# Even-layer forget sums: one scan over 512 tokens for all heads, one product per head over 128 rows

## What is computed

```
logf = log_sigmoid(f_logit + b_f)                  # (token, head)
c    = cumsum(logf, over tokens)
s    = q k^T / 8 + c[query] - c[key]               # causal
y    = softmax(s) v
```

## Time and profile before

| what | value |
|---|---|
| median of 3 runs | 2528.32 us (2528.26 to 2529.1) |
| the profiled execution: its own time | 2530.0 us |
| its span in the trace | 2528.2 us |
| PE busy | 2433.6 us, 96% |
| DVE busy | 1658.5 us, 66% |
| ACT busy | 1168.0 us, 46% |
| mean granted clock of PE | 0.989 |

### The profile page before, as it was taken

One profiled execution on the slowest core, in us unless ns is written; L12 is line 12 of the kernel. 1 busy time (PEld: TensorE's weight loads), 2 busy tenths in 40 slices (PEclk: granted clock), 3 DMA queues, 4 the chain that ended last, 5 costly groups with the idle time before them and its releaser, 6 DMA issues.

```text
span 2528.2 us, 37287 instructions
## 1 busy us (share of the span) xinstructions
PE 2433.6 (96%) x13811; PEld 2151.9 (85%) x13811; DVE 1658.5 (66%) x2733; ACT 1168.0 (46%) x2111; POOL 146.7 (6%) x217
## 2 busy tenths in 40 slices
PE   7999999999999999999999999999988899999998
PEld 5999987886777899987789998777777677999887
DVE  6777647666666877745687774563235868777545
ACT  4455435344445555534545553452223655555444
POOL 1000001100002000001000000100001420000000
PEclk9999999999999999999999999999997999999999
DMA  4333334421304233334423323443244042333345
GB/s 132 98 84 84 109 124 164 117 73 52 111 19 126 74 89 92 89 124 132 159 70 91 92 85 125 133 146 125 79 125 117 9 142 72 93 87 84 108 133 175
DMA packets 259138, 261.87 MB, mean 104 GB/s; under 512 B 25568, under 2 KB 214000, under 8 KB 258977
## 3 DMA queue, kind: packets, MB, share of 16 engines
q1 hardware_dynamic: 254224, 243.83, 31.9%
q0 software_dynamic: 4464, 14.80, 1.7%
q10 hardware_dynamic: 288, 1.10, 0.1%
HBM read 249.11 MB, written 10.58 MB: 103 GB/s over the span
## 4 chain that ended last, share of the span: by engine, by line
PE 83%; DVE 9%; ACT 3%; issue 2%; DMA 1%; POOL 1%; SPq 0%; ACTq 0%; DVEq 0%
PE ps L972 13%; PE ps L973 13%; PE ps L974 13%; PE ps L1030 5%; PE ps L1031 5%; PE ps L1032 5%; PE ps L1443 3%; PE ps L1445 3%; PE ps L1444 3%; PE ps L1089 2%; PE ps L1091 2%; PE ps L1090 2%; PE ps L965 2%; PE ps L1999 1%; PE ps L1650 1%
## 5 line engine op out<-in xcount | busy, mean ns | idle before, releaser
L972 PE MATMUL ps<-xb,w_all 128*128 128x320 f32 x2176 | 673.7, 310 | 8.8 <-ACT scratch L705 6.4
L973 PE MATMUL ps<-xb,w_all 128*128 128x320 f32 x2176 | 673.1, 309 | 0.0
L974 PE MATMUL ps<-xb,w_all 128*128 128x320 f32 x2176 | 673.0, 309 | 0.0
L533 DVE TENSOR_TENSOR w_all<-raw,w_all 128x1024 fp32r<-128x1024 f32 (+1 forms) x204 | 208.0, 1020 | 362.3 <-ACT w_all L543 196.9
L972 PEld LDWEIGHTS ps<-xb,w_all 128*128 128x128 f32 x2176 | 409.0, 188 | 11.7 <-issue 11.7
L974 PEld LDWEIGHTS ps<-xb,w_all 128*128 128x128 f32 x2176 | 409.1, 188 | 0.0
L973 PEld LDWEIGHTS ps<-xb,w_all 128*128 128x128 f32 x2176 | 409.1, 188 | 0.0
L527 ACT ACTIVATE w_all<-raw 128x1024 fp32r<-128x1024 f32 (+1 forms) x204 | 182.5, 895 | 439.2 <-PE ps L1032 237.4
L636 DVE TENSOR_TENSOR w_all<-raw,w_all 128x512 fp32r<-128x512 f32 x364 | 251.5, 691 | 145.4 <-ACT w_all L629 144.5
L629 ACT ACTIVATE w_all<-raw 128x512 fp32r<-128x512 f32 x364 | 229.2, 630 | 182.0 <-PE ps L974 139.2
L1030 PE MATMUL ps<-w_all 128*128 128x512 f32 x528 | 205.9, 390 | 0.9 <-DVE w_all L548 0.9
(11 more groups left out here) (379 smaller groups left out, 4192.8 us busy)
## 6 DMA issues: line engine op xcount, KB each, us to landing
raw<-in_w_ffn_out SPq DMA_DIRECT2D x176, 512.0 KB, 3.3
raw<-in_w_ffn_in SPq DMA_DIRECT2D x120, 512.0 KB, 4.7
gain<-in_w_ffn_in SPq DMA_DIRECT2D x56, 512.0 KB, 4.2
raw<-in_w_in_odd SPq DMA_DIRECT2D x56, 256.0 KB, 2.7
raw<-in_w_out_even SPq DMA_DIRECT2D x16, 512.0 KB, 3.4
raw<-in_w_out_odd SPq DMA_DIRECT2D x16, 512.0 KB, 3.5
gain<-in_norm_g POOLq DMA_DIRECT2D x12, 512.0 KB, 6.6
raw<-in_w_in_even SPq DMA_DIRECT2D x24, 256.0 KB, 2.6
```

Of the source, the lines that this page charges most:

```text
L533: return nc.vector.tensor_tensor(lo, raw[:, RAW[u][0], 0:n], hi.bitcast(F32), ALU.subtract)
L972: nc.tensor.matmul(dst, wl, xh[:, k, :], start=fresh and k == 0, stop=False, skip_group_check=True)
L973: nc.tensor.matmul(dst, wh, xl[:, k, :], start=False, stop=False, skip_group_check=True)
L974: mm = nc.tensor.matmul(dst, wh, xh[:, k, :], start=False, stop=(k == HK - 1), skip_group_check=True)
```

## The change

The sums over tokens are made once for all heads. After unit 20 PE turns the four prompt tiles of `lgn` (128x8) into 8 rows of 512 in bank 7. DVE clears a tile `c_all` of 128x512 (in the place of `w_gate`, whose last reader is done by then) and runs one scan of 8x512 from PSUM into its first 8 rows. After unit 22 PE turns the 8 rows back, in four pieces, into the 32 columns of bank 7, and DVE takes them to `cq` with the sign changed, behind its last weight unit. In the prompt, `sums(h)` becomes one float32 product of 128x512: the stationary operand is column `h` of the identity, broadcast, and the moving one is all 128 rows of `c_all`, of which 120 are zeros.

```diff
@@ views of the arena, behind kTE @@
         w_gate = view(arena, at, CL, 2, P)
+        c_all = view(arena, at, SEQ)
+        c_rows = c_all[0:NH, :]
@@ pe_prompt @@
-                for kb in range(NP):
-                    for b in range(kb + 1):
-                        mm = nc.tensor.matmul(bank(6, P, kb * P), lgn[:, b, h:h + 1].to_broadcast([P, P]),
-                                              con[:, C_UT:C_UT + P] if b == kb else ones,
-                                              start=(b == 0), stop=(b == kb))
-                mm.then_inc(nc_mm, 1)
+                nc.tensor.matmul(bank(6), con[:, C_ID + h:C_ID + h + 1].to_broadcast([P, P]), c_all,
+                                 start=True, stop=True).then_inc(nc_mm, 1)
@@ pe_cumulate @@
             for i in range(NP):
-                for b in range(i + 1):
-                    mm = nc.tensor.matmul(bank(7, NH, 64 + i * NH), con[:, C_UT:C_UT + P] if b == i else ones,
-                                          lgf[:, b, :], start=(b == 0), stop=(b == i))
+                mm = nc.tensor.transpose(ps[0:NH, 7, i * P:(i + 1) * P], lgn[:, i, :], ident)
+            mm.then_inc(lg_ps, 1)
+
+        def pe_cumulate_turn(pe):
+            pe.wait_ge(cum_done, 1)
+            for i in range(NP):
+                mm = nc.tensor.transpose(bank(7, NH, 64 + i * NH), c_rows[:, i * P:(i + 1) * P],
+                                         con[0:NH, C_ID:C_ID + NH])
             mm.then_inc(cq_mm, 1)
@@ pe_between @@
             if m == Q_AT:
+                pe_cumulate_turn(pe)
                 pe.wait_ge(t_out, 10)
@@ dve_even_blocks @@
                 if m == K_AT + 2:
-                    dve.wait_ge(cq_mm, 1)
-                    nc.vector.tensor_copy(cq, bank(7, NP * NH, 64).rearrange("p (t h) -> p t h", h=NH)).then_inc(cq_done, 1)
+                    dve.wait_ge(lg_ps, 1)
+                    link(dve, nc.vector.memset(c_all, 0.0))
+                    nc.vector.tensor_tensor_scan(c_rows, con[0:NH, C_ONE:C_ONE + 1].to_broadcast([NH, SEQ]),
+                                                 ps[0:NH, 7, :], 0.0, ALU.mult, ALU.add).then_inc(cum_done, 1)
                     dve.wait_ge(ya_done, CL)
                     for t in range(NT):
                         dve_tr(dve, t, tile_of(kTE, t))
                     dve_sample_prepare(dve, 0)
+            dve.wait_ge(cq_mm, 1)
+            nc.vector.tensor_scalar(cq, bank(7, NP * NH, 64).rearrange("p (t h) -> p t h", h=NH),
+                                    -1.0, None, ALU.mult).then_inc(cq_done, 1)
             for t in range(NT):
                 dve_tr(dve, NT + t, tile_of(qTE, t))
```

More of the change, by code:

```diff
@@ L296, in build_trunk @@
         cq_mm, cq_done = sem("cq_mm"), sem("cq_done")
+        lg_ps, cum_done = sem("lg_ps"), sem("cum_done")
         conv_done, gate_mm = sem("conv_done"), sem("gate_mm")
```

## The result

The kernel became slower, by 0.6%: 2543.88 us median of 6 runs, against 2528.97 for the kernel before on the same chip (6 runs), a ratio of 1.006 with a 95% interval of 1.0049 to 1.0071. The forecast was 2518.9 with a range up to 2523.5. The runs also spread far more: 2536.74 to 2553.31 us, where those of before lie between 2528.26 and 2529.98. The profiled execution is the fastest of the six (2536.74, span 2534.9; the one of before 2530.0 and 2528.2), so it shows 6.7 us of the 15. The slower runs have no trace, so where they lose the rest is not shown.

What follows compares the result with a forecast made beforehand. PE was taken to bound the kernel, with 83% of the chain of waits. The terms 8.27 + 2.1 - 0.47 - 0.44 gave 9.46 us off the median of 2528.32: 2518.9 us, range 2515.0 to 2523.5.

Steps and rivals of the forecast that it cites:

- that rival: Even prompt loop: PE's clock falls to half once products are taken out; 2571 if held from the second head, chance 0.03.
- the price per low microsecond: At half clock a microsecond of PE work takes two; a stretch of 16.8 us gives back 8.4 us.
- the point of decision: Half-clock stretch in the prompt loop from which the kernel is slower by over 0.2%: 29 us.
- The product: New float32 product of 512 columns in each block: 0.86 us in place of 2.43, so a block shrinks by 1.57.
- my dear bound: Dear end for the new product, from 512 columns over 64 rows: 1.05 us, a gain of 1.38 a block.
- The six blocks in heads: Six blocks inside prompt heads, all else hidden: 9.42 us, or 8.27 after the loss in one head; heads of 7.47 us.
- The head with the weight unit: Prompt head with line 533: DVE runs behind and takes the 512-column scores late, losing 1.15 us of its 1.57.
- The first head: First prompt head, two blocks: 1.33 us from the first, partly at half clock, and 0.75 from the second; 2.1 us.
- The even projections: Ahead of the prompt: DVE's memset and scan delay PE by 0.47 us, the four turns back add 0.44 us.
- The zeros cost or save nothing.: New product in each block: its time goes by columns, so the rows of zeros neither cost nor save time.
- DVE as the limit in every head: Rival: DVE limits every head, each of six blocks gives 0.42 instead of 1.57; 2524.6, no difference, chance 0.12.
- The sum without the clock: Whole kernel: six blocks 8.27 plus first head 2.1, less 0.47 and 0.44 in the projections, 9.46 us off.

Runs made afterwards that it cites:

- e5_eight_rows: Changed kernel with the one product taken over the 8 filled rows alone, in all eight places; 2567.17 us, ratio 1.0154 to the kernel before.
- e6_two: Changed kernel with the 512-column product issued twice in each of the eight places; 2526.34 us, ratio 0.9991 to the kernel before.
- e3_ten_first: Changed kernel with the old ten products for heads 0 and 1, the one product for heads 2 to 7; 2525.98 us, ratio 0.9987 to the kernel before.
- e4_ten_later: Changed kernel with one product for heads 0 and 1, the old ten products for heads 2 to 7; 2529.50 us, ratio 1.0006 to the kernel before.
- e7_turns: Changed kernel with 16 transposes of 128x128 ahead of each product; 2533.77 us, ratio 1.0018 to the kernel before.
- e12_one_late: Changed kernel with the scan behind the sample preparation and no memset, one product a block; 2531.02 us, ratio 1.0017 to the kernel before.

## Why the prediction was wrong

The step that failed is the clock, in the sentence "Against it: no idle time of PE stands in this loop, and none is added", with its chance of 0.03. I had taken idle time ahead of a fall as its condition, from the earlier trace rows, and counted PE's busy time as enough to hold the clock. As a reading it was wrong too: the loop of before has 0.69 us of idle time in the first head and 1.18 in the last. But idle time is not what decides: before kept its clock behind both, and e5_eight_rows lost it at 679.5 us with PE busy for 11.50 of the 11.50 us ahead. The mechanism of that rival, products taken out of the loop, is what happened: the clock was low for 34 us in the profiled execution, and with the product issued twice the low time went from 106 us to 54 and the time from 2543.88 to 2526.34. I had the price per low microsecond nearly right (a half; the heads show 0.45), and the point of decision too: the mean run had 53 us more low time than before, beyond the 29 from which I had put the loss. What I had not seen is that the earlier trace rows already show the other side of the block: in the first head the clock came back during the ten products (674.4, in a block from 670.74 to 674.78). Why the clock stays low for 34 us in one execution and comes back after 3.4 or 6.8 in another stays open.

The other steps, in the order of the text:

- **The product.** Taken at 0.86 us, measured 1.05 at 721.00, my dear bound; only the very first, behind transposes of 128 rows, took 0.87 (670.52). Behind the scores of 64 rows it is the dear one; in e6_two, a second product behind the first makes the block 1.91, 0.86 more. The error is 0.19 us in each of six blocks, and heads took 7.67 in place of 7.47. By the gap of 0.216 us that the Trainium skill, "TensorE: Matmul & The Clock Gate", section "Back-to-back issue gap", gives for one matmul, the product was to take 0.43 us, an estimate; the measured 1.05 is farther from it.
- **The six blocks in heads.** Hidden as forecast: at the full clock the chain is PE's alone.
- **The head with the weight unit.** Forecast loss 1.15 us; e3_ten_first shows 1.05.
- **The first head.** Forecast 2.1 us; 4.2 in the profiled execution (670.52 to 680.94, 10.42 us, against 14.58 from 670.74 to 685.32). That was luck: the low clock ahead of it did not come in this execution, and 1.6 us of the 4.2 is the first block of before at half clock (4.04 us for 2.43).
- **The even projections.** Forecast 0.47 + 0.44 = 0.91 us; 0.61 at the key copies (620.31 for 619.70) and 0.34 for the turn back, and 1.06 by the start of the samples. Of this, 0.18 stood there before anything new had run (DVE's weight work at 617.91 for 617.73), so the change itself costs 0.88. The scan over 8 rows from PSUM took 1.21, as taken from the one of 640. Timeline of DVE of the changed kernel, the answer to the earlier trace rows:

```profile
618.66 0.48 DVE L2417 MEMSET arena<- 128x512 f32 x1
619.18 1.21 DVE L2418 TENSOR_TENSOR_SCAN arena<-con,ps 8x512 f32<-8x512 f32 x1
620.31 1.25 DVE L1548 COPY arena<-ps 128x512 f32<-128x512 f32 x2
...
630.34 0.19 DVE L2425 TENSOR_SCALAR small<-ps 128x32 f32<-128x32 f32 x1 [2.26 <-PE ps L2266]
```

- **"The zeros cost or save nothing."** True of the length of a record, wrong of the kernel: without them it takes 23 us more.
- **DVE as the limit in every head**: did not happen.

The sum without the clock is borne out as far as it can be told: rest by rest, the changed kernel does its work 11.0 us faster (2491.9 against 2502.9), or 8.4 if a low microsecond costs 0.45, where 9.46 was forecast. Terms within it were off both ways, the product by 1.1 us over six blocks and the first head by 2.1 the other way, 1.6 of it luck.

## What to carry to other kernels

Before work is taken from PE in a loop that depends on the full clock, ask what of that work is dense and uses all rows, and what the loop looks like without it; a loop can be shown 100% busy and still be one in which the clock falls and stays low for long (34 us here, 106 with eight rows). Where such a cut is worth making, leave something thick in the place where PE is thinnest (here the first head: low time 61 us with two products there, 106 with one), and compare the mean granted clock of every run, not one profile: a spread of 17 us in place of 2 was the first sign. Padding a short product with rows of zeros cost no time on PE here and paid by the clock.

## What was not expected of the hardware

- Rows count for the clock: three products a block over 8 rows, low 189 us; over 128 rows, of which 120 are zeros, low 59 us; records of nearly the same length at the same clock.
- Float32 transposes of 128x128 count as products do: low 56 us with 16 of them a block.
- The granted clock came back within a thick block at half clock (674.4 before, 686 in e4_ten_later), and also among thin ones after 3.4 and 6.8 us; but it stayed low for 34 us in the changed kernel, and over 8 rows for 106, with PE shown busy throughout.
- The clock fell with no idle time of PE ahead: at 679.5 us in e5_eight_rows, behind 11.50 us of work without a pause.
- A lone float32 product of 128x512 takes 0.87 us behind transposes over 128 rows (0.86 in e7_turns), and 1.05 behind a product over 64.
- The low time varies between runs of one and the same kernel: with clocks between 0.977 and 0.989 e12_one_late took from 2546 to 2522 us.
